# GpSimd makes the remainders of each mixer step's second unit of weights

## The reference

```
for l in range(2):
    x = x + 0.5 * swiglu(rms_norm(x, norm_ffn1[l]), w_ffn1_in[l], w_ffn1_out[l])
    x = x + hybrid_mixer(rms_norm(x, norm_mix[l]), mem, positions, w_in[l], ...)
    x = x + 0.5 * swiglu(rms_norm(x, norm_ffn2[l]), w_ffn2_in[l], w_ffn2_out[l])

hybrid_mixer:
    proj = h @ w_in            # three attentions' inputs, a pooling input, four gates' logits
    o_a, o_c = causal attention with rotary, forgetting attention   (8 heads of 64)
    o_m = attention over 256 memory rows                            (4 heads of 128)
    o_b = means over windows of 2, 4, 8, 16 tokens, mixed and scaled
    y = einsum(stack(o_a, o_b, o_c, o_m), w_branch)
    return sum(sigmoid(gates) * y) @ w_out
```

## Time and profile before

| | |
|---|---|
| median of 3 runs | 1343.31 us (1342.1 to 1343.94) |
| the profiled execution: its own time, its span | 1343.46 us, 1341.6 us |
| busy in the span: PE, PEld, DVE | 1333.8 us (99%), 1103.2 us (82%), 910.9 us (68%) |
| busy in the span: ACT, POOL | 685.1 us (51%), 173.1 us (13%) |
| granted TensorE clock | 1.00 |
| the chain of work that ended last | PE 99% of the span, every other engine and DMA 0% when rounded |
| first mixer, second mixer | from about 187 to 485 us, from about 852 to 1149 us |

### The profile page before, as it was taken

How to read it: one execution, slowest core, us unless ns; L and a number is a source line. 1 busy time by engine, 2 the same in 40 slices (tenths; PEclk the granted TensorE clock), 3 DMA queues, 4 the chain that set the end, 5 groups by cost and what they waited for, 6 DMA issues and landing times.

```text
span 1341.6 us, 15934 instructions
## 1 busy us (share of the span) xinstructions
PE 1333.8 (99%) x6236; PEld 1103.2 (82%) x6236; DVE 910.9 (68%) x1190; ACT 685.1 (51%) x962; POOL 173.1 (13%) x192
## 2 busy tenths in 40 slices
PE   8999999999999999999999999999999999999999
PEld 7888888888888888888888888888888888888887
DVE  5666777778887666656475664876888776665653
ACT  5444455554646455454355454555546544644442
POOL 0334310000000002233003230000000000023320
PEclk9999999999999999999999999999999999999999
DMA  8877665656444547777557675545554545477771
GB/s 306 247 229 220 174 231 175 190 168 215 157 167 157 178 136 238 217 226 221 189 187 221 208 225 196 201 146 172 186 190 157 187 158 176 161 223 226 220 212 63
DMA packets 167852, 260.05 MB, mean 194 GB/s; under 512 B 56657, under 2 KB 66401, under 8 KB 167777
## 3 DMA queue, kind: packets, MB, share of 16 engines
q1 hardware_dynamic: 166592, 255.81, 60.1%
q0 software_dynamic: 896, 3.16, 0.7%
q10 hardware_dynamic: 288, 0.07, 0.0%
HBM read 245.37 MB, written 1.06 MB: 184 GB/s over the span
## 4 chain that ended last, share of the span: by engine, by line
PE 99%; DMA 0%; DVE 0%; ACT 0%; issue 0%; SPq 0%; ACTq 0%; DVEq 0%
PE psum L638 24%; PE psum L902 23%; PE psum L665 21%; PE psum L648 12%; PE psum L907 11%; PE psum L860 1%; PE psum L758 1%; PE psum L776 1%; PE psum L746 1%; PE psum L797 1%; PE psum L864 1%; PE psum L763 1%; PE psum L807 1%; DMA raw<-in_w_ffn_in 0%; PE psum L593 0%; PE psum L845 0%
## 5 line engine op out<-in xcount | busy, mean ns | idle before, releaser
L1322 DVE TENSOR_TENSOR ring_lo<-raw,ring_hi 128x1024 fp32r<-128x1024 f32 x459 | 580.4, 1278 | 342.1 <-ACT ring_hi L973 340.8
L973 ACT ACTIVATE ring_hi<-raw 128x1024 fp32r<-128x1024 f32 x463 | 481.1, 1047 | 570.9 <-PE psum L648 235.4
L638 PE MATMUL psum<-ring_hi,hT 128*128 128x512 f32 x1408 | 348.0, 389 | 2.8 <-DVE hT L1748 1.8
L638 PEld LDWEIGHTS psum<-ring_hi,hT 128*128 128x128 f32 x1408 | 264.1, 188 | 58.2 <-DVE ring_hi L1754 1.9
L902 PE MATMUL psum<-ring_hi,hT 128*128 128x512 f32 x960 | 241.7, 394 | 0.0
L902 PEld LDWEIGHTS psum<-ring_hi,hT 128*128 128x128 f32 x960 | 177.7, 188 | 37.9 <-ACT ring_hi L973 0.7
L648 PE MATMUL psum<-ring_lo,hT 128*128 128x512 f32 x704 | 188.7, 390 | 0.2 <-DVE ring_lo L1742 0.2
L1268 POOL COPY planes<-gate 128x1024 uint16<-128x1024 uint16 (+1 forms) x48 | 68.0, 1445 | 685.6 <-DVE gate L1396 685.6
L648 PEld LDWEIGHTS psum<-ring_lo,hT 128*128 128x128 f32 x704 | 131.8, 188 | 27.7 <-DVE ring_lo L1742 0.6
L907 PE MATMUL psum<-ring_lo,hT 128*128 128x512 f32 x480 | 128.4, 389 | 0.0
L665 PE MATMUL psum<-ring_hi,act_hi 128*128 128x512 f32 x352 | 110.4, 389 | 0.0
(11 more groups left out here) (192 smaller groups left out, 1116.0 us busy)
## 6 DMA issues: line engine op xcount, KB each, us to landing
raw<-in_w_ffn_in SPq DMA_DIRECT2D x78, 1024.0 KB, 5.2
raw<-in_w_in SPq DMA_DIRECT2D x64, 1024.0 KB, 5.1
raw<-in_w_ffn_out SPq DMA_DIRECT2D x44, 1024.0 KB, 5.0
raw<-in_w_branch SPq DMA_DIRECT2D x16, 1024.0 KB, 5.1
raw<-in_w_ffn_in SPq DMA_DIRECT2D x19, 512.0 KB, 4.9
raw<-in_w_mem_kv SPq DMA_DIRECT2D x8, 1024.0 KB, 5.1
raw<-in_w_out SPq DMA_DIRECT2D x8, 1024.0 KB, 5.0
forget<-negc_rows POOLq DMA_DIRECT2D x2, 1024.0 KB, 10.0
```

Of the source, the lines that this page charges most:

```text
L638: pe.matmul(outs[t][:, :], hT[part][:, kc, t * P:(t + 1) * P], w[0][:, kc - first, :], start=kc == 0 and part == 0, stop=False)
L973: act.activation(unit_out(0, step, k), view, ACT.Copy).then_inc(hi_done.sem, 1)
L1322: dve.tensor_tensor(unit_out(1, step, k), view, unit_out(0, step, k).bitcast(F32), ALU.subtract)\
```

## The change

DVE no longer makes the remainder of unit 1 of any mixer step. GpSimd makes it, with the same `tensor_tensor` subtraction, as soon as `hi_done` has the unit. It counts on a new semaphore, `lo_second`; `lo_done` now counts the rest. TensorE's `wait_unit` and SP's `load` wait on the semaphore of the unit in question (SP on both for a mixer step). GpSimd makes those up to step `gate (3, 0)` ahead of its three DMAs, and the others behind them. The feed-forwards keep all their remainders on DVE.

```diff
-        lo_done = tally("lo_done", UNITS, 2 * RAW)
+        lo_done = tally("lo_done", UNITS - len(MIX), 2 * RAW)
+        lo_second = tally("lo_second", len(MIX))
...
+        def remainder_of(L, step, k):
+
+            in_mixer = min(max(step - MIX0, 0), len(MIX))
+            if MIX0 <= step < FFN2_0:
+                if k:
+                    return lo_second.sem, lo_second.at(L, in_mixer + 1)
+                return lo_done.sem, lo_done.at(L, 2 * MIX0 + in_mixer + 1)
+            return lo_done.sem, lo_done.at(L, 2 * step - in_mixer + k + 1)
...
-                sp.wait_ge(lo_done.sem, lo_done.at(L, 2 * (m - RAW) + 2))
+                layer, step = (L, m - RAW) if m >= RAW else (L - 1, m - RAW + STEPS)
+                if layer >= 0:
+                    if MIX0 <= step < FFN2_0:
+                        sp.wait_ge(*remainder_of(layer, step, 0))
+                    sp.wait_ge(*remainder_of(layer, step, 1))
...
-                pe.wait_ge(lo_done.sem, lo_done.at(L, n + 1))
+                pe.wait_ge(*remainder_of(L, n // 2, n % 2))
...
+            def second_remainders(L, kinds):
+
+                for step in kinds:
+                    pool.wait_ge(hi_done.sem, hi_done.at(L, 2 * step + 2))
+                    pool.tensor_tensor(unit_out(1, step, 1), unit_words(step, 1)[1], unit_out(0, step, 1).bitcast(F32), ALU.subtract)\
+                        .then_inc(lo_second.sem, 1)
+
             for L in range(DEPTH):
                 if L:
                     turn_groups(L, 0)
+                second_remainders(L, range(MIX0, _step_of("gate", (3, 0))))
                 pool.wait_ge(negc_ready.sem, negc_ready.at(L, 1))
...
+                second_remainders(L, range(_step_of("gate", (3, 0)), FFN2_0))
                 turn_groups(L, 1)
...
             def lo(L, step, k):

+                if MIX0 <= step < FFN2_0 and k:
+                    return
```

## The result

The median of 4 runs is 1362.01 us (1358.39 to 1368.13), against 1342.84 us (1342.1 to 1343.94, 4 runs) for the kernel before: ratio 1.0148, 95% interval 1.0122 to 1.0174. The change makes the kernel slower by 1.5%. Forecast were 1357.4 us and a range of 1344.5 to 1386.

The account below looks back on a forecast made before the run. TensorE was taken as the bound, busy for 297.90 of 298.00 us in the first mixer. Four holds, 3.1 + 0.7 + 2.5 + 0.75 = 7.05 us a mixer, 14.1 in both, gave 1343.3 + 14.1 = 1357.4 us; range 1344.5 to 1386.

Parts of the forecast that it names:

- the mechanism: In the mixers, a DVE instruction with two SBUF inputs waits for a whole GpSimd subtraction, up to 2.1 us; others don't.
- the small ones: DVE's small two-SBUF-input instructions, such as Newton steps, are held too; if not, the sum is some 9 us.
- cheap or hidden: Rival: GpSimd's subtraction costs close to a copy, 1.04 us; 1.4 us for both mixers, 1344.7 us; chance 0.20.
- dear: Rival: GpSimd's subtraction goes towards 4.2 us, holds twice as long, some 45 us in both mixers, 1388 us; chance 0.20.
- Faster: Rival: DVE's relief is worth what TensorE waits, 0.1 us for each mixer, 1343.1 us; chance 0.03.
- GpSimd's duration: One GpSimd subtraction taken as 2.1 us, two inputs read one behind the other at the copy's pace.
- step 12: First unit's remainder has 0.1 us of slack; holds of Newton steps and remainder cost TensorE 3.1 us a mixer.
- keys' rotary: Unit (24, 1)'s subtraction runs 322.9 to 325.0 and delays L1716 to 327.1; the transposes wait 0.7 us a mixer.
- ahead of scores 3: DVE is gapless with 0.26 us of slack; subtractions delay L1587 and L1605; TensorE loses 2.5 us a mixer.
- share 3: Unit (31, 1)'s subtraction holds L1596 until 371.8, so L776 comes 0.75 us late in each mixer.
- costed at nothing: No cost given to SP's second wait, nor to GpSimd's three DMAs, done by about 317 with unit (24, 1) behind them.
- SP's second wait: In weight loads: costs nothing, as slots of `raw` are released four steps ahead.

Follow-up runs that it names:

- 8: Kernel before, plus three GpSimd memsets for nobody at each of 48 full-size mixer steps, their buffer allocated behind all others: 1342.12 us, ratio 1.0.
- experiment 5: Changed kernel with the mixers' second remainders made by nobody, TensorE multiplying what lies in the ring: 1341.53 us, ratio 0.9995 to the kernel before.
- 1: Changed kernel, but GpSimd makes the second remainder only at steps 12 and 13 of each mixer, DVE the others: 1350.65 us, ratio 1.0064.
- 11: Changed kernel, but GpSimd makes the second remainder only at steps 24 and 25 of each mixer: 1344.45 us, ratio 1.0013.
- 12: Changed kernel, but GpSimd makes the second remainder only at steps 27, 28, 29 and 31 of each mixer: 1349.6 us, ratio 1.0053.
- 6: Changed kernel with each full GpSimd subtraction split into two pieces of 512 elements: 1354.61 us, ratio 1.0099 to the kernel before.
- 2: Changed kernel, but DVE keeps steps 12, 13, 24, 25, 27, 28, 29, 31 and GpSimd makes the other 42 of 50: 1341.9 us, ratio 0.9995.
- quarters: Changed kernel with each full GpSimd subtraction split into four pieces of 256 elements: 1354.66 us, ratio 1.0091 to the kernel before.
- 10: Kernel before with a never used buffer of 128x800 float32 allocated ahead of the two rings: 1362.73 us, ratio 1.0153.
- 3: Kernel before, plus a GpSimd subtraction of 128x800 for nobody at 48 steps of each mixer, its buffer ahead of the rings: 1393.2 us, ratio 1.0379.
- 7: Kernel before, plus a GpSimd subtraction of 128x800 for nobody at 48 steps of each mixer, its buffer behind all others: 1380.66 us, ratio 1.0286.

## Why the prediction was right, and which term it lacked

**The direction and the mechanism** were right: DVE's instructions with two SBUF inputs wait for the whole of a GpSimd instruction that reads SBUF, down to those of 8 elements in a partition; L1720, with an input in PSUM, doesn't; memsets, which only write, hold nobody (8). That the small ones are held too was a conclusion from remainders and copies alone; the 2.40 us Newton step shows it. The rival *cheap or hidden* falls by the duration, 2.4 us, since it needed some 1.3 or less. The *dear* one falls by the same number, since it needed 3 to 4. *Faster* falls by experiment 5.

**GpSimd's duration.** Taken were 2.1 us between bounds of 1.04 and 4.2; it is 2.35 to 2.42 unheld. The estimate of 2.25 us from the Trainium skill (GPSIMD Engine Reference, "Elementwise — side-by-side cycle accounting") was the nearer one. The full units in a mixer are 48, not 46: GpSimd's L1313 has 96 of them in both (the sum by places doesn't use this number).

**The places.**

| place | predicted, a mixer | first, second mixer | alone |
|---|---|---|---|
| step 12 | 3.1 | 2.91, 2.91 | 2.91 (1) |
| keys' rotary | 0.7 | 3.82, 0.65 | 0.65 (11) |
| ahead of scores 3 | 2.5 | 1.87, 1.95 | 0.67 + 1.52 (12) |
| share 3 | 0.75 | 0.45, 0.44 | 0.86 (12) |
| both mixers | 14.1 | 15.0 | 13.2 |

The sum of 14.1 us was 0.9 short, and that it came so close is partly luck: in both mixers together the rotary stage was 3.1 us too low, and the other three places were 2.2 too high. Scores and share are smaller in the full change than alone; that a stall is smaller where TensorE is already late from an earlier one fits this, but wasn't tried by itself. The working ahead of scores 3 also has a slip: its terms, 2.2 + 2.1 - 1.2, give 3.1 us where it says 3.3.

**The rotary stage in the first mixer** is where "costed at nothing" was wrong. The prediction had GpSimd's three DMAs done by then ("from 308.8 to about 317") and let it begin unit (24, 1) at 322.9, 0.6 us after it was rounded. POOL's and DVE's timelines after, with those of the second mixer behind them:

```profile
325.59 0.88 POOL L1324 DMA_DIRECT2D forget<-negc_rows  x1
326.49 2.42 POOL L1313 TENSOR_TENSOR ring_lo<-raw,ring_hi 128x1024 fp32r<-128x1024 f32 x1
330.54 2.38 POOL L1313 TENSOR_TENSOR ring_lo<-raw,ring_hi 128x1024 fp32r<-128x1024 f32 x1 [1.63 <-ACT ring_hi L987]
...
324.95 4.52 DVE L1729 TENSOR_TENSOR qk<-qk,gains 128x512 f32<-128x512 f32 x2
...
330.65 2.43 DVE L1741 TENSOR_TENSOR qk<-qkT 128x128 f32<-128x128 f32 x1
```

```profile
1006.12 3.50 DVE L1729 TENSOR_TENSOR qk<-qk,gains 128x512 f32<-128x512 f32 x2
...
1010.79 0.28 DVE L1741 TENSOR_TENSOR qk<-qkT 128x128 f32<-128x128 f32 x1
...
1011.71 2.75 POOL L1313 TENSOR_TENSOR ring_lo<-raw,ring_hi 128x1024 fp32r<-128x1024 f32 x1 [2.64 <-ACT ring_hi L987]
```

The unit was rounded at 325.03 (ACT L987, 323.97 + 1.06), but GpSimd was issuing the DMAs of `forget` until 326.47, so its subtraction began 1.46 us after the rounding. The second of the pair of L1729 had begun at 325.56 and ended at 329.47, 0.56 us behind the end of that subtraction: the pair took 4.52 us in place of 1.30. DVE was then late enough for the next subtraction (330.54) to hold the last instruction of the stage as well: 2.43 us in place of 0.28. In the second mixer L1741 ended 0.64 us ahead of that subtraction. One hold more or less hangs on a fraction of a microsecond; between the two mixers it makes 3.2 us. With halves (6) it is the same: in the first mixer the last instruction was held too (1.38 us) and the stall was 2.7 us, in the second 0.5. That SP's second wait cost nothing was right (2).

**The missing term is the clock.** The prediction took the granted clock as full throughout: the trace before has no stall in the mixers behind which it could have been read. In the profiled execution each of the five stalls of 1.87 to 3.82 us has the clock at 0.50 for 3.4 or 6.8 us. The run whose clock stayed at 1.000 took 1358.39 us, 1.0 from the forecast; the median has 3.6 us more, and the profiled run 9.7. The four runs, ordered by their clock, differ by these 9.7 us, and those of the kernel before by under 2.

## What to carry to other kernels

A second engine helps only if the first is in the way: ask first what TensorE waits for, and if the answer is nothing, moving work has nothing to gain. GpSimd beside DVE is free where DVE has slack; for each chain of DVE that TensorE awaits, compare its slack with the length of one GpSimd instruction, count every DVE instruction in it that has two inputs in SBUF, however small, and leave GpSimd out of the steps where it doesn't fit (here 42 of 50 units cost nothing). Halves made the hold smaller; quarters gained nothing more, since GpSimd itself came late. And each stall of a busy TensorE should be priced with what the clock may lose at it.

## What the runs showed of the hardware that was not expected

- **The clock falls at short stalls of an engine that is 98% busy, and not always.** Behind stalls of 2.91 us it was 0.50 in one mixer and 1.00 in the other of one execution (1); at a stall of 2.7 us with halves (6) it stayed at 1.00, and at one of 1.87 in the changed kernel it fell. With stalls of up to 1.5 us it never fell in five runs (12). What decides stays open.
- **The place of the buffers is worth 20 us.** A never used buffer of 3200 bytes for each partition, between `hT` and the rings, makes the matmuls that multiply `hT` take 395 ns in place of 389 and leaves those of `act_hi`, which lies behind the rings, as they were (10); behind all others it costs nothing (8). Why was not tried.
- **A hold began before GpSimd's subtraction did, while it issued the DMA ahead of it.** The second instruction of the pair at 324.95 began at 325.56, before the issue of L1324 (325.59 to 326.47) had even started, and could have ended at 326.2, ahead of the subtraction at 326.49. It ended at 329.47, 0.56 us behind that subtraction. The traces have it again: in the first mixer with halves (6: from 324.64 to 328.48, where the two halves end at 327.92) and in both mixers of 3 and 7 (2.8 to 3.0 us in place of 0.68). Beside the same issue the same instruction took its usual 0.68 us where memsets followed the issue (8) and where no subtraction followed at once (2). So the issue alone doesn't hold DVE: it takes a subtraction that reads, right behind it. But the first of the pair ran unheld beside the issue in the second mixer (0.69 us from 1006.12 on, with the subtraction at 1006.57), and no run here shows why the hold can begin so early.
